# Two-layer hybrid decoder step: where the rows of retrieved experts are weighed, on TensorE or on VectorE

## The reference, cut to what matters

```python
g = jax.nn.softmax(best, axis=-1)
act = jax.nn.gelu(jnp.einsum("thkd,td->thk", u_tab[eidx], xb).astype(jnp.float32))
return jnp.einsum("thk,thkd->td", (g * act).astype(xb.dtype), v_tab[eidx])
```

## Time and profile before

| what | value |
|---|---|
| median of 3 runs (lowest to highest) | 5373.72 us (5367.85 to 5380.49) |
| the profiled execution: time, span in the trace | 5361.49 us, 5359.9 us |
| busy share of the span | TensorE matmul 93%, VectorE 54%, GpSimd 35%, ScalarE 18% |
| share of the chain that ended last | TensorE 74%, DMA 8%, issue 6%, VectorE 4% |
| V-tile matmuls (line 1334), two layers | 994.2 us |
| U-tile matmuls (line 1292), two layers | 998.4 us |
| T rows (line 1322), two layers | 384 matmuls of the form from xT, 189.5 us |

### The profile page before, as it was taken

The page is one execution under the profiler, slowest core; times in us unless marked ns, Lnnn a source line. Parts: engine busy times, 40 slices in busy tenths (PEclk is TensorE's granted clock), DMA queues, the critical chain, the costliest instruction groups (busy, mean ns, idle before and its releaser), DMA issues.

```text
span 5359.9 us, 83883 instructions
## 1 busy us (share of the span) xinstructions
PE 5004.6 (93%) x25708; PEld 3891.5 (73%) x25708; DVE 2888.4 (54%) x5803; ACT 966.7 (18%) x2118; POOL 1860.2 (35%) x2605
## 2 busy tenths in 40 slices
PE   7999899798999999999889998987989999999997
PEld 5887776577777765777668877765778777657775
DVE  2543333334889649765236333332358896596643
ACT  1112112111111147100011121121111111570000
POOL 4430001324654526553145200013156444365421
PEclk9999999899999999999999999997999999999998
DMA  7743689566899969998677446886678999699975
GB/s 272 245 169 112 211 252 318 178 229 227 293 333 348 420 228 351 399 419 336 233 264 251 153 125 211 270 288 191 207 253 298 338 354 403 242 352 411 414 297 215
DMA packets 723454, 1489.03 MB, mean 278 GB/s; under 512 B 64592, under 2 KB 405584, under 8 KB 721568
## 3 DMA queue, kind: packets, MB, share of 16 engines
q0 software_dynamic: 249888, 858.18, 43.2%
q1 hardware_dynamic: 473216, 626.61, 34.9%
HBM read 1315.99 MB, written 302.75 MB: 302 GB/s over the span
## 4 chain that ended last, share of the span: by engine, by line
PE 74%; DMA 8%; issue 6%; DVE 4%; DVEq 2%; SPq 2%; POOLq 2%; POOL 1%; ACT 0%; ACTq 0%
PE PS L1292 18%; PE PS L1334 17%; PE PS L685 9%; PE PS L789 8%; PE PS L1223 3%; PE PS L916 3%; PE PS L1242 2%; PE PS L1247 2%; DMA xT<-v_rows,arena 2%; PE PS L1322 2%; PE PS L828 1%; DMA hT<-v_rows,arena 1%; DMA arena<-v_rows,arena 1%; DMA u_rows<-arena 1%; SPq L487 1%
## 5 line engine op out<-in xcount | busy, mean ns | idle before, releaser
L1292 PE MATMUL PS<-hT,ring 128*128 128x288 f32 x4096 | 998.4, 407 | 11.5 <-DMA ring<-in_uv 11.5
L1334 PE MATMUL PS<-arena,ring 128*128 128x288 f32 x4096 | 994.2, 406 | 0.0
L1292 PEld LDWEIGHTS PS<-hT,ring 128*128 128x128 f32 x4096 | 780.6, 191 | 228.5 <-issue 12.4
L1334 PEld LDWEIGHTS PS<-arena,ring 128*128 128x128 f32 x4096 | 777.9, 190 | 216.0 <-issue 1.0
L556 POOL DMA_DIRECT2D u_rows<-arena x1024 | 565.0, 553 | 140.5 <-DVE arena L1484 60.1
L789 PE MATMUL PS<-hT,ring 128*128 128x272 f32 x2304 | 598.9, 406 | 3.6 <-DMA ring<-in_wst 3.6
L789 PEld LDWEIGHTS PS<-hT,ring 128*128 128x128 f32 x2304 | 435.2, 196 | 95.2 <-issue 14.1
L685 PE MATMUL PS<-hT,ring 128*128 128x272 f32 x2048 | 478.1, 393 | 0.0
L1937 DVE CUSTOM_DVE_ANT_0 xT<-xT,PS 128x1024 f32<-128x1024 f32 x340 | 410.6, 1215 | 95.7 <-DMA xT<-u_rows,arena 93.3
L2139 ACT ACTIVATE arena<-PS 128x272 f32<-128x272 f32 (+7 forms) x454 | 186.9, 424 | 1465.1 <-PE PS L789 525.8
L685 PEld LDWEIGHTS PS<-hT,ring 128*128 128x128 f32 x2048 | 385.4, 190 | 77.6 <-issue 0.9
(11 more groups left out here) (394 smaller groups left out, 6210.0 us busy)
## 6 DMA issues: line engine op xcount, KB each, us to landing
ring<-in_uv SPq DMA_DIRECT2D x512, 512.0 KB, 6.4
ring<-in_wst SPq DMA_DIRECT2D x312, 512.0 KB, 5.6
u_rows<-arena POOLq DMA_DIRECT2D x1024, 128.0 KB, 4.6
v_rows<-in_uv SPq DMA_DIRECT2D x256, 512.0 KB, 6.5
arena<-in_uv POOLq DMA_DIRECT2D x216, 512.0 KB, 6.1
arena<-in_ck SPq DMA_DIRECT2D x128, 256.0 KB, 5.4
arena<-in_cvv POOLq DMA_DIRECT2D x64, 256.0 KB, 4.7
hT<-in_cvv POOLq DMA_DIRECT2D x64, 256.0 KB, 5.1
```

Source lines behind the costliest of these rows:

```text
L1292: i = mm(PS[:, 2 + s % 2, 0:TD], ring[:, s, c, :], hD[:, c, :], start=(c == 0), stop=(c == DC - 1))
L1334: i = mm(PS[:, 2 + b, 0:TD], ring[:, s, j, :], WB[:, row, :], start=(row == 0), stop=(row == NK - 1))
```

## The change

Three things change, together with the bookkeeping for them.

1. A row is taken on each side only in every second group of the one-hot stage. TensorE takes a T row, and ScalarE makes a diagonal, in even groups (`N_DG` = 36 instead of 72). VectorE takes a dot in odd groups (36 instead of 72). The one-hot work of the 72 groups is the same. 16 more dots of block 1 (`N_EARLY` 48 for 32) come before the stage. The 36 v rows that TensorE no longer takes go to VectorE, with line 1950's multiply-and-add, after the stage.
2. The exponential stands behind U tile 80 instead of 92.
3. The switch of the four buffers (`N_SW`) is at row 498 instead of 486, so the last 14 rows, 12 of them behind TensorE's release, are fetched behind the switch instead of 26. VectorE waits for x after row 505, and the seven residual updates share the last six rows.

```diff
-    for g in range(N_OH):
+    for g in range(N_DG):
         order += [v[0][g], u[1][N_EARLY + g]]
-    return order + u[1][N_EARLY + N_OH:] + v[0][N_OH:] + v[1]
-N_EARLY = 32
+    return order + u[1][N_EARLY + N_DG:] + v[0][N_DG:] + v[1]
+N_EARLY = 48
 N_OH = TD // 4
+N_DG = N_OH // 2
-N_SW = (NROW - 24) // NBUF * NBUF
+N_SW = (NROW - 12) // NBUF * NBUF
...
                 i.then_inc(oh_mm.sem, 1)
-                n = T_ROWS[g]
+                if g % 2:
+                    continue
+                r = g // 2
+                n = T_ROWS[r]
...
                     i = mm(HTK[0][:, hf, :], DG[r % 2], row_buf(n)[:, hf * 512:(hf + 1) * 512], start=(r == 0), stop=(r == N_DG - 1))
...
-                row()
+                if g % 2:
+                    row()
...
-            rows(RANK[N_SW + NBUF + 5])
+            rows(RANK[N_SW + NBUF + 1])
...
-                row()
+                rows(min(at + 1, len(V_ROWS)))
...
-            dots(68, 92)
+            dots(68, 80)
             s_.wait_ge(tk_v.sem, tk_v.at(l, 1))
             act(GW, GW, ACT.Exp).then_inc(sx_e.sem, 1)
...
-            dots(92, NK)
+            dots(80, NK)
...
             for g in range(N_OH):
                 if 0 < g < N_OH - 1:
                     row_onehots(g + 1)
+                if g % 2:
+                    continue
+                r = g // 2
-                if g >= 2:
-                    s_.wait_ge(row_t.sem, row_t.at(l, g - 1))
-                act(DG[g % 2], ident[:, :], ACT.Copy, scale=DOT[:, g:g + 1]).then_inc(dg_s.sem, 1)
+                if r >= 2:
+                    s_.wait_ge(row_t.sem, row_t.at(l, r - 1))
+                act(DG[r % 2], ident[:, :], ACT.Copy, scale=DOT[:, r:r + 1]).then_inc(dg_s.sem, 1)
```

More of the change, by code:

```diff
@@ L164, in row_order @@
     order = u[0] + u[1][:N_EARLY]
-    for g in range(N_OH):
+    for g in range(N_DG):
         order += [v[0][g], u[1][N_EARLY + g]]
-    return order + u[1][N_EARLY + N_OH:] + v[0][N_OH:] + v[1]
-N_EARLY = 32
+    return order + u[1][N_EARLY + N_DG:] + v[0][N_DG:] + v[1]
+N_EARLY = 48
 N_OH = TD // 4
+N_DG = N_OH // 2
 ROWS = row_order()
 NROW = len(ROWS)
-N_SW = (NROW - 24) // NBUF * NBUF
-on_tensor = lambda n: ROWS[n][0] == "v" and ROWS[n][1] == 0 and ROWS[n][2] < N_OH
+N_SW = (NROW - 12) // NBUF * NBUF
+on_tensor = lambda n: ROWS[n][0] == "v" and ROWS[n][1] == 0 and ROWS[n][2] < N_DG
 T_ROWS = [n for n in range(NROW) if on_tensor(n)]
@@ L403, in build @@
     row_v, row_t = Sig("row_used_by_vector", len(V_ROWS)), Sig("row_used_by_tensor", len(T_ROWS))
-    dot_s, dot_v, dg_s = Sig("dots_activated", 2), Sig("first_row_weights_ready", 1), Sig("row_diagonal_ready", N_OH)
+    dot_s, dot_v, dg_s = Sig("dots_activated", 2), Sig("first_row_weights_ready", 1), Sig("row_diagonal_ready", N_DG)
     xk_st, xr_ld = Sig("x_kept", 16), Sig("x_loaded_again", 16)
@@ L1315, in _ @@
                 i.then_inc(oh_mm.sem, 1)
-                n = T_ROWS[g]
+                if g % 2:
+                    continue
+                r = g // 2
+                n = T_ROWS[r]
                 pe.wait_ge(row_ld[n % NBUF].sem, row_ld[n % NBUF].at(l, 16 * (n // NBUF + 1)))
                 pe.nop(nofuse=True)
-                pe.wait_ge(dg_s.sem, dg_s.at(l, g + 1))
+                pe.wait_ge(dg_s.sem, dg_s.at(l, r + 1))
                 pe.nop(nofuse=True)
                 for hf in range(2):
-                    i = mm(HTK[0][:, hf, :], DG[b], row_buf(n)[:, hf * 512:(hf + 1) * 512], start=(g == 0), stop=(g == N_OH - 1))
+                    i = mm(HTK[0][:, hf, :], DG[r % 2], row_buf(n)[:, hf * 512:(hf + 1) * 512], start=(r == 0), stop=(r == N_DG - 1))
                 i.then_inc(row_t.sem, 1)
@@ L1940, in row @@
                 else:
-                    if blk == 0 and k == N_OH:
-                        v.wait_ge(row_t.sem, row_t.at(l, N_OH))
+                    if blk == 0 and k == N_DG:
+                        v.wait_ge(row_t.sem, row_t.at(l, N_DG))
                         v.nop(nofuse=True)
```

## The result

The changed kernel takes 5325.28 us (median of 5 runs, 5308.66 to 5336.16), the kernel before 5373.72. The ratio is 0.9904, 95% interval 0.9877 to 0.9931: 0.96% faster, or 52 us by the ratio and 48 by the medians, clearly more than the 0.2% that can be told from no change. Predicted were 5309 us in a range of 5286 to 5345. The profiled execution took 5330.14 us with a span of 5328.6, at a mean granted clock of 0.964 as before.

The account below looks back on a forecast made before the run. TensorE, busy 93% of the span, was taken to bound the kernel. Gains of 20.5 us (one-hot stage) and 11.7 us (layer's end) per layer, 64.4 for two, off the median 5373.7 gave 5309 us, range 5286 to 5345.

Parts of the forecast that it names:

- The one-hot stage: From first one-hot matmul to first V matmul: predicted 197.1 us instead of 217.6, 20.5 us less per layer.
- the loop: One-hot stage: waits from one-hot matmul through Abs, diagonal and T row to the next matmul, 5.39 us per pair.
- The fullest engine as pace (4.47): Rival, one-hot stage: VectorE's 4.47 us sets the pair, stage 164.9 us, kernel 5245 us; chance 0.06.
- The clock: One-hot stage: TensorE's granted clock might fall through idling, making a pair 7.95 us; forecast expected 1.00; chance of falling 0.07.
- The slower rival: TensorE's clock falls in the one-hot stage: stage 286.7 us, kernel 5488 us, slower than before; chance 0.07.
- The dots ahead of the stage: 16 more dots in VectorE's 68.0 us wait before the one-hot stage: take 30 us, leave 38, cost nothing.
- The exponential: Instruction moved to behind U tile 80: ScalarE's wait 22 us from biting, predicted cost zero.
- The ladder: VectorE's rows in the V stage, set by fetches at 1.865 us each: predicted gain 11.7 us per layer.
- head start: Rows already landed at V start: taken as 3.5 of six buffers, bounds 0 and 6, against none before.
- the predicted sum (64.4): 20.5 us from the one-hot stage plus 11.7 from the V stage's end, 32.2 a layer, 64.4 for two.

Follow-up runs that it names:

- diagonal first: Changed kernel, but ScalarE makes an even group's diagonal ahead of the next group's one-hots instead of behind them: 5251.19 us, ratio 0.9762.
- 64 early dots: Changed kernel with 64 instead of 48 dots of block 1 ahead of the one-hot stage: 5294.81 us, ratio 0.9844.

## Why the prediction was right, and where a size was off

- **The one-hot stage.** Right in mechanism and size. Predicted 197.1 us, measured 196.6 and 197.7; pair 5.39 predicted, 5.38 measured; idle before each T row 1.6 predicted, 1.65 measured, with the diagonal as releaser. That the loop is the cause is shown by breaking it (31 us less).
- **The fullest engine as pace (4.47).** Wrong for the changed kernel, right for the one with the diagonal first. The rule of the Trainium skill, "Perfetto Trace Analysis", section "Identifying the Most-Contended Engine", would have named VectorE as what to optimise first here, at 81% of the stage the busiest; the runs put the cause in ScalarE's order.
- **The clock.** The granted clock was 0.99 over the stage, though TensorE idled 1.65 us in every 5.39. Only the first ten microseconds were at 0.80 (before 0.74), with a first T row of 3.41 us. The slower rival is out.
- **The dots ahead of the stage.** Predicted to leave 38 us of VectorE's wait, measured 37.3 (it was 68.0 in the earlier trace rows). Nothing was lost.
- **The exponential.** Predicted zero, measured zero. U tile 80's GELU is at 1758.27, the exponential's table load at 1758.70, without a wait.
- **The ladder.** This is the term that was mis-sized: "three to four of the six have landed, while before it was none", counted as 3.5 rows of head start over before. Predicted gain 11.7 us a layer, measured 7.4 and 7.2 of TensorE's idle; that is 8.8 of the 9.8 us by which the predicted sum (64.4) exceeds the measured one (54.6). The rest of the chain was right: from row 499 to the copy 36.3 us predicted, 35.7 measured; 208 v rows at 1.868 us.

What was wrong with the head start can be read from the rows after V start. Of the changed kernel:

```profile
2145.90 1.22 DVE L1941 CUSTOM_DVE_ANT_0 xT<-xT,PS 128x1024 f32<-128x1024 f32 x1
...
2151.60 1.22 DVE L1941 CUSTOM_DVE_ANT_0 hT<-hT,PS 128x1024 f32<-128x1024 f32 x1
...
2154.20 1.22 DVE L1941 CUSTOM_DVE_ANT_0 xT<-xT,PS 128x1024 f32<-128x1024 f32 x1 [1.36 <-DMA xT<-u_rows,arena]
...
2226.59 2.69 DVE L1950 SCALAR_TENSOR_TENSOR PS<-xT,arena,PS 128x1024 f32<-128x1024 f32 x2 [1.24 <-DMA xT<-v_rows,arena]
```

The 44 u rows from V start to the first v row took 81.1 us, and before the change 24 took 46.0: the 20 rows more cost 35.1 us, 2.2 less than at 1.865, so the head start was worth 1.15 rows against the 3.5 that I took.

The count of landed rows was right. Six dots follow each other 1.14 us apart and wait for nothing, but not all six rows had landed at V start (2145.46). GpSimd had issued them at 2133.15, 2135.97, 2138.54, 2141.36 and 2143.93, and the sixth only after V start:

```profile
2146.75 0.94 POOL L665 DMA_INDIRECT hT<-u_rows,arena  x1 [1.89 <-DVE arena L1941]
```

At the 4.5 us that a fetch took in this stage, three had landed and the fourth nearly. What was wrong is the other side: before, rows on their way counted too. Three dots ran there without a wait behind V start (2165.46), on rows issued 1.9 to 5.0 us before it, and the fourth waited:

```profile
2169.19 1.22 DVE L1937 CUSTOM_DVE_ANT_0 hT<-hT,PS 128x1024 f32<-128x1024 f32 x1
2171.29 1.22 DVE L1937 CUSTOM_DVE_ANT_0 hT<-hT,PS 128x1024 f32<-128x1024 f32 x1 [0.86 <-DMA hT<-u_rows,arena]
```

So the changed kernel is three rows ahead at its first wait, but that wait ends 8.7 us after V start for 5.8 before, which takes 2.9 us, or 1.6 rows, of it back. With the diagonal first, where a row is asked for every 2.2 us and not every 2.7, the picture is the same (six dots, then a wait that ends 8.9 us after V start). The windows of the first two tens of microseconds after V start, of the changed kernel and then of before:

```profile
2145.50:2155.50 10.00, 10.00 (x41) 7.85 (x42) 8.56 (x16) 0.00 (x0) 6.56 (x7) 1.00 0.82 259
2155.50:2165.50 10.00, 10.00 (x43) 7.84 (x42) 5.24 (x9) 0.00 (x0) 3.74 (x4) 1.00 1.02 413
```

```profile
2165.50:2175.50 10.00, 10.00 (x43) 7.85 (x42) 8.38 (x14) 0.00 (x0) 6.80 (x8) 1.00 1.01 377
2175.50:2185.50 10.00, 10.00 (x43) 7.85 (x42) 6.49 (x11) 0.00 (x0) 4.70 (x6) 1.00 1.02 417
```

Rows that have landed are no longer being moved, and a new fetch starts only when a buffer comes free. In the first 10 us the changed kernel moved 259 GB/s where it moved 413 in the next ten, 1.5 MB or 2.9 rows less; before it was 377 of 417, 0.4 MB or 0.8 rows. So part of the head start was lost again in transfers that weren't asked for yet. This reading rests on rows alone, and no run of its own tested it; how the 2.35 rows between 3.5 and 1.15 divide between rows in flight before and transfers not asked for after stays open.

What stays open: the measured medians lie up to 11 us beyond the sums of the table (64 early dots -82.7 for -71.6). The mixer's length differs by up to 25 us from one profiled execution to the next. That would be enough for it, but no run shows that it is the cause, and which of the mixer's transfers differ wasn't followed further than the cache pages.

## What to carry to other kernels

When a change takes work off every engine of a stage and none is full afterwards, look for a circle of waits through two engines: add up the spacings from one instruction to its next turn, and try the order inside the one queue that sits in the circle before taking away more work. Where a stream paces a stretch, a row moved out of it is worth its full transfer time only until the next wait (here TensorE's release) takes over, so find how much slack each side has before adding two gains. And value a head start against the kernel before: rows that were in flight there count too, and rows that have already landed also mean that fewer transfers are under way when the busy stretch begins.

## What the runs showed of the hardware that was not expected

- An indirect fetch of 512 KB took 4.4 to 4.7 us from issue to landing in the changed kernel's one-hot stage (188 GB/s), 5.9 us in that of before (336 GB/s, and the earlier trace rows) and 8.8 us in the V stage (417 GB/s). The answers for the changed kernel, one-hot stage and then V stage:

```profile
xT<-u_rows,arena POOLq DMA_INDIRECT x26, 4.5
```

```profile
ring<-in_uv SPq DMA_DIRECT2D x78, 512.0 KB, 6.5
xT<-v_rows,arena POOLq DMA_INDIRECT x102, 8.8
```

- With the tile stream (6.5 us for 512 KB there) beside them, the core moved 417 GB/s over the 300 us from 2200 of the changed kernel, at one row every 1.87 us. VectorE was then busy about 69% and GpSimd 50% of the time, whose issue of one fetch took 0.94 us.
